# Every second group of cached values in the decode attention multiplied unsplit in full precision, the low parts of the others on VectorE alone

## The reference, cut to what matters

```python
def moba_combine(q, q_pos, k_own, v_own, own_pos, ks=None, vs=None, sel_valid=None):
    ...
    p = jax.nn.softmax(jnp.concatenate([ls.reshape(b, h, nq, nk * bs), lo], axis=-1), axis=-1)
    ...
    return (jnp.einsum('bhqkl,bhqkld->bhqd', p_sel.astype(vs.dtype), vs, preferred_element_type=F32)
            + jnp.einsum('bhql,bhld->bhqd', p_own.astype(v_own.dtype), v_own, preferred_element_type=F32))

def gated_delta_chunked(q, k, v, g, beta, s0):
    ...
    t_inv = lax.linalg.triangular_solve(a + eye, jnp.broadcast_to(eye, a.shape),
                                        left_side=True, lower=True, unit_diagonal=True)
    ...
    xs = tuple(jnp.moveaxis(t, 2, 0) for t in (qc, kc, u, w, gc, qk))
    s_fin, o = lax.scan(step, s0, xs)
```

## Time and profile before

| | us |
|---|---|
| median of 3 runs | 1194.81 |
| lowest, highest | 1193.85, 1203.77 |
| profiled execution, its own time | 1196.35 |
| profiled execution, span of its instructions | 1194.5 |
| stage of the change, from the first `sums` product to the last `turn_values` | 403.4 to 623.4 |
| PE busy over the whole span | 1087.3 (91%) |
| mean granted clock | 0.938 of 2.4 GHz |

### The profile page before, as it was taken

One profiled execution on the slowest core, in us unless ns is written; L12 is line 12 of the kernel. 1 busy time (PEld: TensorE's weight loads), 2 busy tenths in 40 slices (PEclk: granted clock), 3 DMA queues, 4 the chain that ended last, 5 costly groups with the idle time before them and its releaser, 6 DMA issues.

```text
span 1194.5 us, 21266 instructions
## 1 busy us (share of the span) xinstructions
PE 1087.3 (91%) x8054; PEld 1013.5 (85%) x8054; DVE 648.0 (54%) x892; ACT 468.7 (39%) x707; POOL 256.4 (21%) x113
## 2 busy tenths in 40 slices
PE   6999899698988589879968999999999999999997
PEld 6999799665677479668758799999999999999997
DVE  5228987897725774676544426555433433433443
ACT  6423554324333544554534122234413413523443
POOL 0035566776300353353330000000000000000000
PEclk8999899858998899989978899999999999999999
DMA  8376777655410245644547115433333332223311
GB/s 283 93 238 197 247 222 208 202 163 169 139 38 1 53 141 150 178 132 141 161 135 190 53 44 170 127 105 89 89 89 89 99 96 88 88 88 90 100 56 72
DMA packets 179256, 152.67 MB, mean 128 GB/s; under 512 B 8913, under 2 KB 141723, under 8 KB 178918
## 3 DMA queue, kind: packets, MB, share of 16 engines
q1 hardware_dynamic: 137414, 124.72, 35.5%
q10 hardware_dynamic: 41768, 26.91, 7.9%
HBM read 142.77 MB, written 8.93 MB: 127 GB/s over the span
## 4 chain that ended last, share of the span: by engine, by line
PE 76%; DVE 11%; ACT 5%; issue 4%; POOL 2%; ACTq 1%; DVEq 0%; POOLq 0%
PE ps L416 57%; PE ps L1795 6%; PE ps L1782 3%; DVE lg L1029 2%; POOL v_low L574 2%; PE ps L1682 1%; PE ps L1696 1%; DVE w_low L405 1%; PE ps L1539 1%; PE ps L1672 1%; ACTq L390 1%; DVE v_low L1261 1%; ACT v_high L827 1%; PE ps L1902 1%; ACT w_high L400 1%
## 5 line engine op out<-in xcount | busy, mean ns | idle before, releaser
L400 ACT ACTIVATE w_high<-w_raw 128x1024 fp32r<-128x1024 f32 x125 | 132.5, 1060 | 423.1 <-PE ps L416 399.8
L416 PE MATMUL ps<-xh,w_high 128*128 128x256 f32 x1216 | 257.5, 294 | 13.3 <-DVE w_low L405 7.4
L405 DVE TENSOR_TENSOR w_low<-w_raw,w_high 128x1024 fp32r<-128x1024 f32 x125 | 160.4, 1284 | 193.9 <-ACT w_high L400 193.6
L416 PE MATMUL ps<-xl,w_high 128*128 128x256 f32 x1216 | 250.0, 288 | 0.0
L416 PE MATMUL ps<-xh,w_low 128*128 128x256 f32 x1216 | 249.6, 287 | 0.0
L416 PEld LDWEIGHTS ps<-xh,w_high 128*128 128x128 f32 x1216 | 193.3, 194 | 21.1 <-issue 20.2
L416 PEld LDWEIGHTS ps<-xl,w_high 128*128 128x128 f32 x1216 | 193.7, 193 | 0.0
L416 PEld LDWEIGHTS ps<-xh,w_low 128*128 128x128 f32 x1216 | 193.6, 193 | 0.0
L557 POOL TENSOR_TENSOR ring<-ring,qb 128x1024 f32<-128x1024 f32 x64 | 158.5, 2488 | 158.7 <-DMA ring<-in_cache_k 87.0
L416 PE MATMUL ps<-mh,w_high 128*128 128x256 f32 (+1 forms) x640 | 129.3, 283 | 2.4 <-issue 2.4
L416 PE MATMUL ps<-mh,w_low 128*128 128x256 f32 (+1 forms) x640 | 129.5, 284 | 0.0
(11 more groups left out here) (358 smaller groups left out, 1498.0 us busy)
## 6 DMA issues: line engine op xcount, KB each, us to landing
ring<-in_cache_k SPq DMA_DIRECT2D x128, 256.0 KB, 3.0
ring<-in_cache_v SPq DMA_DIRECT2D x128, 256.0 KB, 2.9
w_raw<-in_w_in ACTq DMA_DIRECT2D x74, 256.0 KB, 4.0
w_raw<-in_w_up SPq DMA_DIRECT2D x64, 256.0 KB, 3.1
w_raw<-in_w_down SPq DMA_DIRECT2D x64, 256.0 KB, 2.9
w_raw<-in_w_in SPq DMA_DIRECT2D x16, 256.0 KB, 7.4
w_raw<-in_w_out SPq DMA_DIRECT2D x16, 256.0 KB, 3.0
ht_dram<-ht ACTq DMA_DIRECT2D x1, 2080.0 KB, 14.2
```

What stands on the lines that cost most here:

```text
L400: act.activation(w_high[:, u % 2], w_raw[:, s], ACT.Copy).then_inc(S_hi, 1)
L405: dve.tensor_tensor(w_low[:, u % 2], w_raw[:, u % 4], w_high[:, u % 2].bitcast(F32), ALU.subtract).then_inc(S_lo, 1)
L416: last = pe.matmul(out[:, a:b], w[:, u % 2, k, :], x[:, i, a:b], start=(first + i == 0 and w is w_high and x is rhs_h), stop=(first + i == ...
```

## The change

Even groups stay split. They use both buffers of `v_high` and `v_low` among themselves (index g // 2 % 2). Their low part is made by DVE alone. ACT runs three groups ahead at the start instead of one, and waits for the matmuls of group g - 4. Odd groups are not split: PE multiplies `ring` itself with two float32 matmuls, whose weights are the 8 columns of `lg` of that sample and page, 16 elements apart; they are summed into rows 0 to 7 of the same bank. The slot of an even group is free when its low part is made, that of an odd group when its matmuls are done.

```diff
-        def low_done(i):
-            return S["v_low_dve" if i % 2 else "v_low_pool"], i // 2 + 1
+        def slot_free(i):
+            return (S["pv_done"], i + 1) if i % 2 else (S["v_low_dve"], i // 2 + 1)
...
@@ sync, stream and the loads of sample 0
-                        taken, count = low_done(r + 4)
-                        sp.wait_ge(taken, b * 4 + (count - 4))
+                        taken, count = slot_free(r + 4)
+                        sp.wait_ge(taken, b * (8 if r % 2 else 4) + (count - (8 if r % 2 else 4)))
...
@@ gpsimd: values() and its three calls are gone
-                    if i % 2 == 0:
-                        g.wait_ge(S["v_high_out"], i + 1)
-                        g.tensor_tensor(v_low[:, i % 2], ring[:, i % 4].rearrange("p g c -> p (g c)"),
-                                        v_high[:, i % 2].bitcast(F32), ALU.subtract).then_inc(S["v_low_pool"], 1)
...
@@ scalar
-                    act.wait_ge(kv_landed[i % 4], 32 * (2 * NS + i // 4 + 1))
-                    if i >= 2:
-                        act.wait_ge(S["pv_done"], i - 1)
-                    A(v_high[:, i % 2], ring[:, i % 4].rearrange("p g c -> p (g c)"), ACT.Copy)\
-                        .then_inc(S["v_high_out"], 1)
+                    if i % 2 == 0:
+                        act.wait_ge(kv_landed[i % 4], 32 * (2 * NS + i // 4 + 1))
+                        if i >= 4:
+                            act.wait_ge(S["pv_done"], i - 3)
+                        A(v_high[:, i // 2 % 2], ring[:, i % 4].rearrange("p g c -> p (g c)"), ACT.Copy)\
+                            .then_inc(S["v_high_out"], 1)
...
-            values(1)
+            values(3)
...
@@ vector, lows
-                    if i % 2:
-                        v.wait_ge(S["v_high_out"], i + 1)
-                        TT(v_low[:, i % 2], ring[:, i % 4].rearrange("p g c -> p (g c)"),
-                           v_high[:, i % 2].bitcast(F32), ALU.subtract).then_inc(S["v_low_dve"], 1)
+                    if i % 2 == 0:
+                        v.wait_ge(S["v_high_out"], i // 2 + 1)
+                        TT(v_low[:, i // 2 % 2], ring[:, i % 4].rearrange("p g c -> p (g c)"),
+                           v_high[:, i // 2 % 2].bitcast(F32), ALU.subtract).then_inc(S["v_low_dve"], 1)
...
@@ tensor, values
-                    pe.wait_ge(*low_done(g))
...
+                    if r % 2:
+                        pe.wait_ge(kv_landed[g % 4], 32 * (2 * NS + g // 4 + 1))
+                        for i in range(2):
+                            last = mm(bank(2 + b % 2, WB, HB), lg[:, b, :, 2 * r + i], ring[:, g % 4, i, :],
+                                      start=False, stop=(r == 7 and i == 1), skip_group_check=True)
+                    else:
+                        pe.wait_ge(S["v_low_dve"], g // 2 + 1)
...
```

More of the change, by code:

```diff
@@ L339, in hybrid_step @@
             mh_out ml_out h_out sq2_out ssum_ready hx_h hx_l rel_out relsq_out uu_ready uh_out ul_out yt_turned
-            hw_out yf_sums yf_root yf_inv ys_out ys_done y_act y_dve v_scaled vb_masked vb_turned vb_out diag_out v_high_out v_low_pool v_low_dve""".split()
+            hw_out yf_sums yf_root yf_inv ys_out ys_done y_act y_dve v_scaled vb_masked vb_turned vb_out diag_out v_high_out v_low_dve""".split()
         S = {n: sem(n) for n in names}
@@ L505, in _ @@
                 else:
-                    sp.wait_ge(*low_done(r - 4))
+                    sp.wait_ge(*slot_free(r - 4))
                 for i in range(2):
@@ L565, in wide @@
                 return bc(ap.rearrange("p (h o) -> p h o", o=1), [P, HA, DA])
-            values_done = [0]
-            def values(n):
-                for i in range(values_done[0], min(values_done[0] + n, GROUPS)):
-                    if i % 2 == 0:
-                        g.wait_ge(S["v_high_out"], i + 1)
-                        g.tensor_tensor(v_low[:, i % 2], ring[:, i % 4].rearrange("p g c -> p (g c)"),
-                                        v_high[:, i % 2].bitcast(F32), ALU.subtract).then_inc(S["v_low_pool"], 1)
-                values_done[0] += n
-            values(1)
             for stage, c in delta_order():
-                values(VALUES.get(stage.rstrip("0123456789"), 0))
                 if stage == "turn":
@@ L594, in _ @@
                     g.tensor_tensor(k, k, wide(ckb[:, c]), ALU.mult).then_inc(S["k_ready"], 1)
-            values(GROUPS)
             g.wait_ge(S["ys_out"], 1)
@@ L1778, in values @@
                         pe.wait_ge(*done("wz_low"))
[L1779 to L1785, removed]
+                    if r % 2:
[5 more added lines that the diff above has]
+                        pe.wait_ge(S["v_low_dve"], g // 2 + 1)
+                        for i in range(2):
+                            first = (b * NPAGE + 2 * r + i) * 2 * HB
+                            for v_part in (v_high, v_low):
+                                last = mm(bank(2 + b % 2), wz[:, first:first + P],
+                                          v_part[:, g // 2 % 2, i * WB:(i + 1) * WB],
+                                          start=(r == 0 and i == 0 and v_part is v_high), stop=False,
+                                          skip_group_check=True)
                     last.then_inc(S["pv_done"], 1)
```

## The result

The changed kernel takes 1218.41 us (median of 4 runs, 1214.21 to 1219.32) against 1194.33 for the kernel before in the same measurement: ratio 1.0189, 95% interval 1.0159 to 1.0219. It is slower by 1.9%; the forecast was 1191.5 with a range to 1205.

What follows compares the result with a forecast made beforehand. TensorE was taken as the bound in two full stretches of the delta-rule stage, with waits in three others; 25.9 us of added matmul time against recovered waits and clock summed to -3.3 us, 1191.5 from 1194.8, range 1181 to 1205.

Steps and rivals of the forecast that it cites:

- What bounds the kernel: Delta-rule stage: TensorE bounds two full stretches; three others wait; 31.4 us of idleness and 14.9 of low clock can be won.
- The price of an unsplit group: TensorE, odd groups: two float32 matmuls take 1.83 us with the wait, 0.81 more each, 25.9 over 32 groups.
- What it removes: POOL loses 32 low parts (80.3 us), ACT 32 copies (33.6); only the waits they cause count, three come off.
- the lock: VectorE and POOL share a port exclusively; without a lock the sum would be some 4 us worse.
- Edits at nothing, SP's new wait: Even group's load queued on SP behind an odd slot: 6.8 us including its parts, covered by five groups' distance, costing nothing.
- the walk: Five stretches of the stage, longer groups against recovered waits: -5.3, +4.1, -0.6, +4.6, -6.1, sum -3.3 us.
- The third rival: Value loads into the ring late by 0.7 us at some 18 groups: +5 us, 1200; chance 0.10.
- The slower rival: Last stretch stays at 1.2 GHz and unsplit matmuls cost 1.08 more per odd group: +11.4 us, 1206; chance 0.20.
- The range: Whole kernel time: 1181 to 1205 us, leaving out about 1 in 10 on each side.

Runs made afterwards that it cites:

- lead 1: The changed kernel with ScalarE running one group ahead of TensorE at the start instead of three; 1193.12 us, 0.9971 of the kernel before.
- its control: The changed kernel with SyncE's value loads written out without loops in the old order; 1217.75 us, 1.0197 of the kernel before.
- lead 2: The changed kernel with ScalarE running two groups ahead at the start instead of three; 1194.16 us, 0.9979 of the kernel before.
- even load first: The changed kernel, three groups ahead kept, SyncE's loads written out with each even group's ahead of the odd one's before it; 1198.19 us, ratio 1.0010.
- copy last: The changed kernel, three groups ahead kept, ScalarE copying a value group after its own work of the stage; 1203.20 us, 1.0057 of the kernel before.

## Why the prediction was wrong, by its own steps

- **What bounds the kernel.** Right: two full stretches, where every microsecond put on TensorE was paid, and three with waits.
- **The price of an unsplit group.** 1.83 forecast. Measured 1.82: from 432.29 to 434.11 in the timeline above, and the same at nearly every odd group at full clock. The 8 columns of weights saved nothing: 0.91 for 512 streamed columns, against the 0.89 that the prediction read from its rows with 128. Per odd group the full stretches grew by (46.7 - 41.5) / 6 = 0.87 and (50.4 - 44.6) / 6 = 0.97 with lead 1, where 0.81 was forecast; all of this together is 1.3 us. By the four passes of the Trainium skill, "FP8 and Floating Point Precision", section TensorE Precision Notes, two float32 matmuls of 512 columns are an estimated 1.71; the trace's 1.82 is 0.1 above that.
- **What it removes.** Right in its rows: no low part on POOL, L1312's successor at 684 ns throughout, TensorE's waits for low parts 4.4 us. The prediction put the lock at some 4 us on the path. With the low parts back on POOL the stage was 3.9 us longer and the wait ahead of it 3.1, but that holds POOL's longer low part too, so the 4 is not confirmed by itself. That VectorE is slowed beside POOL agrees with the exclusive lock of the Trainium skill, "SBUF — State Buffer", section Who interferes with whom: 1764 ns against 684.
- **Edits at nothing, SP's new wait.** This is the step that failed. It said that two loads and the next two land within some 4.5 us, and that five groups' distance, 5 x 3.4 us, covers it. Both halves were wrong, and the 4.5 had no row of its own. The path is 7.3 us, 434.1 to the landing at 441.4: 0.9 until SyncE's first issue, then issues 1.17 to 1.25 us apart, three of them, then 2.8. And I measured the distance to TensorE's matmuls. The first to need the group is ScalarE's copy, three groups ahead of them by `values(3)`, which leaves a distance of about two groups; at group 12 it asked 1.0 us before the matmuls of group 7 ended. I had entered that lead in the walk as pure gain ("two groups ahead") and did not ask what is queued behind a copy that waits. What stood there instead of nothing: 107.3 us of ScalarE waiting for landings, 15.0 of TensorE waiting for ScalarE, and 23.8 us of stage against the same kernel with the lead of one. The trace of before held the spacing of the issues (403.30 and 404.39 for the first two); I took the landing time alone.
- **The third rival** named the ring, but with TensorE as the waiting engine, 0.7 us at 18 groups, and gave it 5 us and a chance of 0.10. Place right, consumer wrong, size about a fifth of the 23.8 us.
- **The walk.** With lead 1 it holds in the main: five stretches 34.3, 46.7, 56.2, 50.4, 31.8 against 34.6, 45.6, 59.4, 49.2, 27.9. But the stage is 219.4 against 216.6 forecast, only 0.5 us shorter than before instead of 3.3. That the time, 0.9971 of before, is 3.5 us less (0.5 to 6.3), close to the 3.3 forecast, is luck: most of it doesn't lie in the stage. The two stretches furthest off are the last, where group 62's low part still waited, and the middle one, where the clock stayed at 1.00 though I had left it low.
- **The slower rival** (low clock at the end, dearer matmul) did not occur by its own signs. The step is 1.82, not over 2.0. The last stretch's clock did stay low, 0.87, but not behind a wait at the turned output of chunk 3, which is gone: TensorE stood 3.72 us at `new_v` of chunk 3 for `Dm` (L856), which ScalarE made behind another copy that waited for its landing. The time that it gave, 1206, is 12 short.
- **The range.** It ended at 1205 with "about 1 in 10" above, while the chance of over 1206.8 stood at 0.17; the two don't agree.

Shown by runs are the lead, the order of the loads (with its control) and the queue in program order, each by a change of it alone. A total wait of ScalarE of 36 us (lead 2) costs almost nothing because TensorE hardly meets it: 1.3 us of TensorE's idle time ended on ScalarE. Not explained is the difference between even load first and copy last, 8.5 us of stage at 5.6 and 6.1 us of such waits: 5.4 of it is idle time, mostly waits for VectorE, and 3.2 busy time for the same work; no run tests where these come from.

## What to carry to other kernels

When the release of a buffer moves later, follow the load to its first reader, not to the engine that bounds the kernel, and count every issue of the queue on the way; if the first reader runs ahead in an in-order queue, its wait is everybody's behind it. A longer but less dependent form of an operation is worth using where its engine waits and costs its full price where it is full: here the same edit gained 13 us in 20 places and cost 12 in 12 others.

## What the runs showed of the hardware

- SyncE's dynamic loads are issued 1.16 to 1.26 us apart inside the loop, though an issue itself is drawn as 0.33 us; a group of two takes the queue 2.4 us. Written out without the loop they stand 1.09 us apart, which changed nothing in the stage (243.9 against 243.2 us).
- 512 streamed float32 columns take 0.91 us with 8 columns of weights, against some 0.89 with 128 and 1.02 with 64: the narrow weights saved nothing. The weight load is shorter: 95 ns in the mean against 200 for the 128 columns of the split groups.
- A VectorE operation of 128 x 512 with two inputs in SBUF takes 684 ns alone and 1764 to 1982 ns in the mean with GpSimd's low parts beside it.
